# Memory keys and values in float32r high and low parts, the low parts made beside the gated feed-forward and kept in device memory

## The reference, cut to what matters

```python
mem_n = rmsnorm(mem, norm_memsrc_g[l])                 # 256 x 1024
k = (mem_n @ w_k).reshape(B, MEM_LEN, MEM_HEADS, MEM_HEAD_DIM)
v = (mem_n @ w_v).reshape(B, MEM_LEN, MEM_HEADS, MEM_HEAD_DIM)
...
u = h @ w_pw1 + b_pw1                                  # conv module: 1024 -> 2048
a, gate = jnp.split(u, 2, axis=-1)
u = a * jax.nn.sigmoid(gate)
u = lax.conv_general_dilated(u, w_dw[:, None, :], ...)  # 31 taps for each feature
u = jax.nn.silu(layernorm(u + b_dw, ln_g, ln_b)) @ w_pw2 + b_pw2
```

## Time and profile before

| | |
|---|---|
| timed runs | 2259.63, 2259.78, 2260.44 us; median 2259.78 us |
| the profiled execution's own time | 2260.11 us |
| its span | 2258.3 us, so 1.8 us lie around it |
| busy | PE 99%, DVE 57%, ACT 41%, POOL 17% |
| granted TensorE clock | 0.998 of full speed |
| gated feed-forward | about 417 to 774 us |
| convolution's tiles | about 774 to 966 us |
| layernorm and the pair that starts `conv_pw2` | about 966 to 1010 us |

### The profile page before, as it was taken

How to read it: one execution, slowest core, us unless ns; L and a number is a source line. 1 busy time by engine, 2 the same in 40 slices (tenths; PEclk the granted TensorE clock), 3 DMA queues, 4 the chain that set the end, 5 groups by cost and what they waited for, 6 DMA issues and landing times.

```text
span 2258.3 us, 32580 instructions
## 1 busy us (share of the span) xinstructions
PE 2235.7 (99%) x10884; PEld 1825.9 (81%) x10884; DVE 1293.1 (57%) x1859; ACT 930.6 (41%) x1439; POOL 392.8 (17%) x329
## 2 busy tenths in 40 slices
PE   8999999999999999999999999999999999999998
PEld 6777788888888898878888888887777888888887
DVE  5557756543444658865564544585555646454455
ACT  6775644442234545553332222244544333222222
POOL 2232101201010446723040000040000304000003
PEclk9999999999999999999999999999999999999999
DMA  4222223333334434412123333332221223333332
GB/s 149 66 66 63 78 75 99 109 100 93 101 94 119 114 103 130 131 47 84 57 84 103 93 93 102 93 90 75 57 66 57 84 61 89 95 94 100 99 94 87
DMA packets 395666, 202.96 MB, mean 90 GB/s; under 512 B 13808, under 2 KB 393200, under 8 KB 395568
## 3 DMA queue, kind: packets, MB, share of 16 engines
q1 hardware_dynamic: 394672, 199.34, 30.2%
q0 software_dynamic: 896, 2.33, 0.3%
HBM read 199.00 MB, written 2.10 MB: 89 GB/s over the span
## 4 chain that ended last, share of the span: by engine, by line
PE 96%; ACT 2%; DVE 1%; issue 1%; DVEq 0%; DMA 0%; ACTq 0%; SPq 0%
PE bank L1827 26%; PE bank L1829 26%; PE bank L1828 25%; PE bank L2209 3%; PE bank L2201 2%; PE bank L1807 2%; PE bank L2298 1%; PE bank L2275 1%; PE bank L1980 1%; PE bank L2404 1%; PE bank L2371 1%; PE bank L2118 1%; PE bank L2120 1%; PE bank L2119 1%; PE bank L2041 1%
## 5 line engine op out<-in xcount | busy, mean ns | idle before, releaser
L635 ACT ACTIVATE m_w_hi<-m_raw 128x1024 fp32r<-128x1024 f32 x332 | 351.4, 1058 | 822.5 <-PE bank L1829 817.8
L1827 PE MATMUL bank<-m_h_hi,m_w_hi 128*128 128x512 f32 x1504 | 608.4, 405 | 2.0 <-DVE m_w_lo L1164 1.0
L1829 PE MATMUL bank<-m_h_hi,m_w_lo 128*128 128x512 f32 x1504 | 587.2, 390 | 0.0
L1828 PE MATMUL bank<-m_h_lo,m_w_hi 128*128 128x512 f32 x1504 | 586.6, 390 | 0.0
L1164 DVE TENSOR_TENSOR m_w_lo<-m_raw,m_w_hi 128x1024 fp32r<-128x1024 f32 x332 | 448.4, 1351 | 110.5 <-ACT m_w_hi L635 106.9
L1827 PEld LDWEIGHTS bank<-m_h_hi,m_w_hi 128*128 128x128 f32 x1504 | 282.7, 188 | 73.3 <-issue 11.2
L1829 PEld LDWEIGHTS bank<-m_h_hi,m_w_lo 128*128 128x128 f32 x1504 | 282.4, 188 | 60.0
L1828 PEld LDWEIGHTS bank<-m_h_lo,m_w_hi 128*128 128x128 f32 x1504 | 283.0, 188 | 55.5 <-issue 2.4
L1827 PE MATMUL bank<-m_f_hi,m_w_hi 128*128 128x512 f32 x688 | 268.9, 391 | 0.2 <-DVE m_w_lo L1164 0.2
L1829 PE MATMUL bank<-m_f_hi,m_w_lo 128*128 128x512 f32 x688 | 267.9, 389 | 0.0
L1828 PE MATMUL bank<-m_f_lo,m_w_hi 128*128 128x512 f32 x688 | 267.9, 389 | 0.0
(11 more groups left out here) (388 smaller groups left out, 3052.3 us busy)
## 6 DMA issues: line engine op xcount, KB each, us to landing
m_raw<-in_ff_w SPq DMA_DIRECT2D x256, 256.0 KB, 3.0
m_raw<-in_conv_pw_w SPq DMA_DIRECT2D x48, 256.0 KB, 3.9
m_raw<-in_w_in SPq DMA_DIRECT2D x47, 256.0 KB, 3.1
m_raw<-in_w_ffn_gate SPq DMA_DIRECT2D x44, 256.0 KB, 3.1
m_raw<-in_w_ffn_up SPq DMA_DIRECT2D x44, 256.0 KB, 3.2
m_raw<-in_w_ffn_down SPq DMA_DIRECT2D x40, 256.0 KB, 2.9
m_raw<-in_w_gate SPq DMA_DIRECT2D x32, 256.0 KB, 2.9
m_mem_w<-in_mem_wk SPq DMA_DIRECT2D x32, 256.0 KB, 3.0
```

Source lines behind the costliest of these rows:

```text
L635: act.activation(WH[:, v % 2], RAW[:, v % 2], ACT.Copy).then_inc(s.w_hi, 1)
L1827: pe.matmul(o, high[:, r, k, :], hi, start=start, stop=False)
L1828: pe.matmul(o, high[:, r, k, :], lo, start=False, stop=False)
L1829: last = pe.matmul(o, low[:, r, k, :], hi, start=False, stop=stop)
```

## The change

The 32 memory products are now made of float32r parts, like the units: high by high, high by low, low by high. A key product (now on bank `SBK[3]`) has 24 matmuls of 256 columns. A value product is now a quarter (2 of the 8 k) of a 512 wide half of the values, for both blocks of memory rows, with the weights as the moving side: 12 matmuls of 512 columns (banks `SBK[1]` and `SBK[2]`), and ACT copies the two banks out after every fourth.

The low parts of the memory weights are made in the feed-forward: for each of the 32, SP loads the raw weight into one of three slots (`SW`), ACT rounds it into one of two (`SWH`), DVE subtracts in place, and SP writes the low part to a device tensor `mem_low`; one of them every two units, from the fifth unit of the feed-forward to its last. Later SP loads raw weight and low part together (twice 512 KB for a product, into four slots and a fifth at the end), and ACT makes the high part once more (`mem_high`) next to the products. The normed memory has a high part (one buffer, made anew for layer 1 at tile 5, `MEM_TURN`) and a low part for each layer. At tile 0 there are now four memory products, three at each later tile, seven behind the last. ACT makes 13 products of taps and DVE 18. Some loops of ACT, DVE and SP are written out.

```diff
-SUM_TAPS = 12
+SUM_TAPS = 13
+MEM_SPLIT_FIRST = 4
+MEM_TILES = ((0, 4),) + tuple((3 * m + 1, 3 * m + 4) for m in range(1, KD))
+MEM_TURN = 5
+MEM_SLOT = [i % 4 for i in range(MEM_UNITS - 3)] + [2, 3, 4]
...
+            def mem_load(i):
+                w = MEM_SLOT[i]
+                if MEM_NTH[i] > 0:
+                    sp.wait_ge(s.mem_done, i - MEM_SLOT[i - 1::-1].index(w))
+                mem_raw(i, MW[w], mw_in[w])
+                sp.dma_start(MWL[w][:].bitcast(F32), mem_low[i]).then_inc(mw_in[w], 16)
...
+            def split_high():
+                i, odd = divmod(U.n - 1 - ffn - MEM_SPLIT_FIRST, 2)
+                if odd or not 0 <= i < MEM_UNITS:
+                    return
+                act.wait_ge(sw_io[i % 3], 32 * (i // 3) + 16)
+                if i >= 2:
+                    act.wait_ge(s.sw_lo, i - 1)
+                act.activation(SWH[i % 2][:], SW[i % 3][:], ACT.Copy).then_inc(s.sw_hi, 1)
...
             def conv_steps(m):
...
                     products(m - 1, 0, SUM_TAPS // 2)
+                    mem_out(MEM_TILES[m - 1][1] - 1)
+                if m == MEM_TURN:
+                    act.wait_ge(s.mem_done, MEM_LAYER)
+                    for k in range(KD):
+                        memory_high(k, 1)
                 step(None)
+                for i in range(*MEM_TILES[m]):
+                    mem_high(i)
+                if m > 0:
                     products(m - 1, SUM_TAPS // 2, SUM_TAPS)
                 step(None)
...
+            for i in range(MEM_TAIL, MEM_TAIL + 3):
+                mem_high(i)
+            mem_out(MEM_TAIL - 1)
+            products(KD - 1, 0, SUM_TAPS_LAST // 2, SUM_TAPS_LAST, PE_TAPS_LAST)
+            mem_high(MEM_TAIL + 3)
+            products(KD - 1, SUM_TAPS_LAST // 2, SUM_TAPS_LAST, SUM_TAPS_LAST, PE_TAPS_LAST)
+            for i in range(MEM_TAIL, MEM_TAIL + 4):
+                mem_out(i)
+            for i in range(MEM_TAIL + 4, MEM_UNITS):
+                mem_high(i)
...
+                for m in range(KD):
+                    step(residual(m, final, None, gains, base))
+                    gained(m, gains, base)
+                    if final:
+                        memory_low(m, 0)
+                    split_low()
...
-                cut = [0, 8, 14, DVE_TAPS]
+                cut = [0, 8, 13, DVE_TAPS]
...
+            def mem_product(i):
...
+                    for k in range(KD):
+                        for a, b in ((high, MNH), (high, low_mn), (low, MNH)):
+                            last = pe.matmul(SBK[3][:, 0:MEM], a[:, k, :], b[:, k, :],
+                                             start=(k == 0 and a is high and b is MNH), stop=(k == KD - 1 and a is low))
```

More of the change, by code:

```diff
@@ L440, in _, with mem_source @@
             square(W["w_out"][0])
[L441 to L447, removed]
+            def mem_source(i):
+                layer, q, key = mem_unit(i)
+                if key:
+                    return W["mem_wk_2"][layer][:, :, q * P:(q + 1) * P]
+                return W["mem_wv_2"][layer][:, 2 * (q % 4):2 * (q % 4) + 2, q // 4 * T:(q // 4 + 1) * T]
@@ L448, in _, with ffn_unit @@
+            def mem_load(i):
[4 more added lines that the diff above has]
+                sp.dma_start(MWL[w][:].bitcast(F32), mem_low[i]).then_inc(mw_in[w], 16)
+            def ffn_unit(name, m, k0=0, nk=KD):
+                splits()
+                unit(W[name][0], m * P, k0, nk)
             for g0, tiles in ((0, 8), (8, 8), (16, 6)):
[L449 to L452, removed]
+                for m in range(g0, g0 + tiles):
+                    ffn_unit("w_ffn_gate", m)
+                    ffn_unit("w_ffn_up", m)
@@ L453, in _ @@
                 if g0 == 16:
[L454 to L457, removed]
+                    for i in range(2):
+                        mem_load(i)
+                for m in range(KD):
+                    ffn_unit("w_ffn_down", m, g0, tiles)
             def conv_loads(m):
-                unit(W["conv_pw1_w_2"][0], m * P)
@@ L461, in conv_loads @@
[L461 to L470, removed]
+                for half in (0, D):
+                    splits()
+                    unit(W["conv_pw1_w_2"][0], m * P + half)
@@ L927, in _ @@
[L927 to L940, removed]
+                else:
+                    act.wait_ge(s.ff_lo, FF1_TILES)
+                    act.wait_ge(s.mem_normed, KD)
@@ new lines, in _, with mem_high @@
+                gains = [(COL["norm_mix_g_2"], HH, HL)]
+                for m in range(KD):
+                    if done < FF1_TILES:
+                        step(None)
+                    else:
+                        step(lambda bank, free: gained(m, gains), [lambda: memory_high(m, 0)])
+                    split_high()
+            finals[0] += KD
+            def mem_high(i):
+                w = MEM_SLOT[i]
+                act.wait_ge(mw_in[w], 32 * (MEM_NTH[i] + 1))
+                act.activation(MWH[w][:], MW[w][:], ACT.Copy).then_inc(s.sw_hi, 1)
@@ L956, in conv_steps @@
             def conv_steps(m):
-                first = isinstance(m, int) and m == 0
-                q = 0 if first else m * 3 + 3
-                if first:
+                if m == 0:
                     norm()
@@ L987, in _ @@
             last_diagonals()
[L988 to L993, removed]
+            for m in range(1, KD):
+                conv_steps(m)
+            for i in range(MEM_TAIL, MEM_TAIL + 3):
[5 more added lines that the diff above has]
+            for i in range(MEM_TAIL, MEM_TAIL + 4):
+                mem_out(i)
+            for i in range(MEM_TAIL + 4, MEM_UNITS):
+                mem_high(i)
             for k in range(KD):
```

297 lines of the change are left out of this document (180 added, 117 removed).

## The result

The changed kernel takes 2282.46 us (median of four runs, 2282.17 to 2286.37) against 2260.06: 22.4 us more, ratio 1.0103, interval 1.0091 to 1.0116. The forecast was 2276, so the time moved the way that was forecast, by 22.4 us instead of 16.5.

A forecast was written before the change was run, and what follows sets the result against it. Convolution tiles had two equal bounds, PE and a loop through ACT, POOL and DVE, so PE's saved 23.8 us idle. 2260.1 + 7 + 2.3 + 7.4 = 2276.8, profiled run 0.3 above median: 2276 us, range 2252 to 2289.

The forecast's parts named there:

- A: Last down group: DVE's added low parts and splits make the tile pitch 5.1 us; about +7 us, bounds +2 and +11.
- B: Tiles of the convolution: first loop ends earlier (-9.9), six longer loops (+8.6), tile of `MEM_TURN` (+3.6); sum +2.3 us.
- C: Tail, last write of `UP` to the first unit of `conv_pw2`: later squares and ACT's copies; +7.4 us, upper bound +11.
- the forecast case: Whole kernel: A, B and C within their near bounds, 2270 to 2282 us; chance 0.42.
- the loop follows PE: Rival for the convolution's tiles: a tile takes PE's 20.3 us, and the time is 2252 us; chance 0.16.
- Loads: ... none late: Convolution tiles: 4 MB in 23.7 us, 170 GB/s of some 290, hidden; or each tile's third late by 1 to 2 us.
- Squares at G+23.5: Tail: high parts wait for loads, so squares start 23.5 us after the last write of `UP` instead of 17.3; +6.2 us.
- G: End of the last write of `UP`, at 966.2 us in the kernel before; the tail's times count from it.
- The chain behind them keeps its length: Tail, first square to the pair's first matmul: stays 15.3 us, with 1 us more for ACT's copies.

The follow-up runs named there:

- experiment 3: Changed kernel with nothing added to the last down group: layer 0's low parts beside the third group's hidden tiles, splits every 5/3 units; 2274.23 us.
- experiment 1: Changed kernel with 12 products on ACT and POOL instead of 13 (DVE makes 19 taps); 2273.51 us.
- experiment 2: Kernel before with 13 products (18 taps on DVE) and nothing else of the change; 2268.56 us, ratio 1.0037.
- experiment 4: Changed kernel with the high parts of the last two products behind ACT's squares instead of ahead of them; 2275.80 us.
- 6: Changed kernel with 11 products (DVE 20 taps), nothing added to the last down group, and the last two high parts behind the squares; 2254.83 us.
- 8: Changed kernel with the edits of 6, raw weights issued ahead of each tile's third memory load, and three moves on ACT; 2248.93 us, ratio to before 0.995.
- 12: Changed kernel with all edits of 8, but 12 products instead of 11; 2253.06 us.
- experiment 7: Changed kernel with SP issuing the raw weights of a tile's units ahead of the third load of memory weights; 2279.02 us.
- experiment 9: Changed kernel with layer 0's normed memory low and high parts beside the third group's hidden tiles; four splits stay in the last down group; 2282.61 us.
- 10: Changed kernel with the 32 splits every 5/3 units, none in the last down group; the normed memory's low parts stay there; 2280.71 us.

## Why the prediction was nearly right

Its steps against the profiled execution, each a difference to the kernel before, in us:

| step | forecast | measured |
|---|---|---|
| start of the last down group | 0 | +0.5 (746.28) |
| A, first to last write of the stream | +7 | +7.3 (36.4 for 29.1) |
| B, from there to the first product | -11.6 | -11.0 (24.8 for 35.8) |
| B, from there to the second `UP` | +1.7 | +4.7 (25.6 for 21.0) |
| B, six loops | +12.2 | +11.6 (145.5 for 133.8) |
| C, last `UP` to the first square | +6.2 | +9.6 (27.7 for 18.1) |
| C, from there to the pair | +1.2 | +3.7 (19.0 for 15.3) |
| the rest | 0 | -0.1 |
| sum | +16.7 | +26.3 |

The median, 2282.5 us, lies inside the stated range of 2252 to 2289, and just above the forecast case's own 2270 to 2282. The mechanism was right at each of the three places; two of its waits came out at another size than the forecast's. The splits of the feed-forward ahead of its last down group cost nearly nothing (it starts 0.5 us later), and the three stretches that cost something were each taken back by an edit of their own: A by experiment 3, the loops by 1 and, in the kernel before, 2, the tail by 4. The rival that ended on the other side, that the loop follows PE, fell by experiment 2. The loop's added sum was worth what was forecast, 1.43 us: 1.44 in the kernel before (23.69 less 22.25) and 1.45 in the changed one (23.28 less the 21.83 of experiment 1). That the clean loop of the changed kernel is 23.3 and not the forecast 23.7 is another thing: the rest of the change made the loop 0.4 us shorter, with 12 products (21.83 for 22.25) as with 13. Two rows make most of it: the sum that DVE's first split stretches takes 2.08 us in the changed kernel and 2.30 before, and the first product starts 0.78 us behind the start of the write of `UP` instead of 0.97. DVE's wait is 3.34 us there and not 4.8, since the loop is shorter and the first split is stretched too (2.17 us for 1.21). PE is idle for 2.0 us and not 3.4 in the clean loop, in part because one product is 1.7 us longer at the lower clock.

Tile 5 took 3.3 us more than a clean one, forecast 3.6, and the way was the forecast one: POOL waits for ACT's product 6, with the new high parts on ACT's list ahead of it, and DVE still waits for ACT ahead of its second split.

```profile
918.84 1.29 POOL L676 TENSOR_TENSOR m_tap_sum<-m_tap_sum,m_tap_product 128x512 f32<-128x512 f32 x1 [4.20 <-ACT m_tap_product L1038]
```

```profile
924.77 2.22 DVE L1253 TENSOR_TENSOR m_w_lo<-m_raw,m_w_hi 128x1024 fp32r<-128x1024 f32 x1 [2.24 <-ACT m_w_hi L699]
```

The forecast said nothing of DVE's eight low parts in that tile (5.3 us). They fit because DVE had room: 2.24 us of it is left. With 12 and 11 products it is gone, which is why that tile stayed at 25 us in experiments 1, 6, 8 and 12. That two of the other five loops are 24.4 us and not 23.3 made up for the difference.

Three terms were too small, together by 8.9 us of the profiled execution's 9.6:

- "Loads: ... none late" was wrong. The queue's mean of 170 GB/s was no reason, because SP's list is in order: a memory load waits for `mem_done`, and the raw weights, whose slots had been free, stand behind it. That was +3.0 in the first loop, and 1.1 us at each of two tiles. In the trace of experiment 7, with the raw weights ahead, it is gone (2.7 us of the first loop, and the two tiles).
- "Squares at G+23.5": 26.9. The products ahead of the last mean ended later than assumed, so the loads were issued at G+16 to 17 and not from G+13, and the last mean came at G+18.4 and not G+16.
- "The chain behind them keeps its length": it was 3.7 us longer. PE had stood idle and came back at half the clock, which is 2.0 of it (from the first square to the first product behind them, 10.2 us for 8.2). The other 1.7 are the third product ahead of the pair, 8.8 us for 7.1, which the forecast had not counted; no run shows the 1 us that it took for ACT's copies instead. In experiment 4, at the full clock, the chain is still 1.4 us longer than before (16.7 us, 997.57 to 1014.28).

The forecast's A rested on 5.1 us of pitch, between bounds of 4.5 and 5.9; 5.20 was measured. The Trainium skill, page "SBUF — State Buffer", section "🔬 SBUF: two separate sides", calls the shared ports an exclusive lock, and the forecast's estimate by it, for which it shows no working, was 5.3 us and A +9. The pitch lies midway between the two, and A, +7.3, is nearer to the milder sharing. The rows of single instructions agree with the lock, though. In those shown above DVE's instruction ends behind POOL's by a little less than it takes alone: `m_mn_lo` 0.3 us (0.47 alone), `m_h_lo` 0.5 (0.74), and the split of experiment 9 1.1 (1.21). So nearly all of it was done after POOL's had ended.

Some sums of the forecast don't come out as written, without changing its outcome. DVE's 27.94 us leave 5.1 of 33, not 6.1. Pitches of 4.5 and 5.9 would make A +3 and +13, not +2 and +11. Twenty-four times 0.118 and twelve times 0.227 make 88.9 us for the 32 products and a relief of 23.4. What stands ahead of product 6 at `MEM_TURN` adds up to 8.9 us, not 9.3, which would be +3.2. And 6.2 and 1 make 7.2, where the tail was entered with 7.4.

The profiled execution is 3.9 us above the median. The other three weren't profiled, so which of the terms is smaller in them stays open. The tail is a candidate: in the traces of experiments 1, 3, 7, 9 and 10, whose tail is the same, the first square comes 24.7 to 27.2 us behind the last write of `UP`, and 27.7 here. That the loads make this difference is only argued.

## What to carry to other kernels

Where the busiest engine is busy for 99%, look for a second loop of the same period before its work is cut: if one exists, the cut gives nothing there, and most of what it costs the loop is paid (8.4 of 9.9 us in experiment 2). Work that is moved into DVE's idle time has to be priced with POOL's instructions beside it, and a load by what its wait holds up behind it in the queue. And a cut of the busiest engine becomes worth something only together with the edits that shorten the loop: here some 23 us of PE's work, with the down group, the sums, the loads and the order of ACT mended, gave 11.1.

## What the runs showed of the hardware

- After 8.2 us without a matmul, PE ran at a granted clock of 0.50 for the next 5 us, and a float32 matmul on a square took 1.87 us from start to start instead of 0.96. In tiles of the changed kernel with a wait of PE of 2 us and more, the clock's mean was 0.85 to 0.95, and behind a wait of 2.03 us matmuls of 512 columns came every 0.43 us instead of 0.23. Idle time on the engine that was the bound so costs a second time when work comes back.
- The wait for POOL is passed on: without `m_mn_lo` the next instruction, a split, went from 1.21 to 2.31 us. Of 8.2 us of the group that two edits gave together, one gave 2.7 alone and the other 4.2 (in the medians of the whole time, 1.8 and nothing, within a spread of 3 and 7 us).
- The kernel before repeats within 1.6 us over all its runs; the changed one and its relatives spread by 1.6 to 7.4 us. That SP's queue and the loop, which wait for one another there, make this spread is not shown.
